# 544 tokens cut 256/288, with the high and low inputs of 256 tokens in one 512-column matmul

## Chip, cores and metric

One Trainium2 chip; the kernel runs on one of its cores. The metric is the device time of one execution in microseconds (us).

## What is computed

A trunk of two layers over 544 tokens (512 of a new stream, the prompt, and 32 of a running one, the sample), each of 1024 features, in float32:

```python
def layer(x, c, l, mixer):
    mods = (silu(c) @ ada_w[l] + ada_b[l]).reshape(c.shape[0], 9, D_MODEL)   # D_MODEL 1024
    h = modulated_pre(x, norm_pre[l, 0], mods, 0)          # rms_norm * (1 + scale) + shift
    x = gated_post(x, swiglu(h, w1, w3, w2), ...)          # D_FF 2816: (silu(h@w1) * (h@w3)) @ w2
    h = modulated_pre(x, norm_pre[l, 1], mods, 1)
    o, st = mixer(h, l)                                    # z = h @ w_in; latent attention | retention; @ w_out
    x = gated_post(x, o, norm_post[l, 1], mods, 1, 1.0)
    h = modulated_pre(x, norm_pre[l, 2], mods, 2)
    x = gated_post(x, swiglu(h, ...), ...)                 # a second FFN
```

## The kernel before

Activations lie feature-major: 128 features on the partitions, 8 tiles of them, 544 tokens along a row. A projection is made one output tile of 128 features at a time. To keep float32 precision with TensorE's faster float32r type, each operand is split into a high part (rounded to float32r) and a low part (the rest), and each product is three matmuls: high weights by high input, high weights by low input, low weights by high input. No matmul writes more than one PSUM bank of 512 float32, so the 544 tokens are cut in two halves of 272 (`HT`), which lie in two neighbouring banks. `tile3` does one step of 128 input features: six matmuls, `w_hi` by `hi` and `lo` for either half, then `w_lo` by `hi` for either half. In the up projection of the FFN and the mixer's input projection the second half has 276 columns (`HB`): the last four hold the adaLN shift of prompt and sample, so that the product with the shift comes out as a bias beside the tokens, to be added after the scaling with 1/rms (`rinv`).

The stages of a layer: FFN (44 up tiles in 22 features with two tiles each, w1 and w3; then 8 down tiles of 22 steps), mixer (21 input tiles z0 to z20, query projections, retention and attention, 8 output tiles), and a second FFN. Between stages lies a turn-over: the sum of squares of the output, its inverse root, the new x, the next h. The last output tile of a stage is made one token half after the other (`last_tile`), and the first two tiles of the next (`first_tiles`) start with the first half, so that the turn-over of one half lies beside the matmuls of the other. The halves are always the same 272 tokens.

Each engine has its own program, in an order written by hand, and they wait for each other on semaphores:

- SyncE's queue loads the weights of a tile into one of two slots of `raw`.
- ScalarE casts a slot to `w_hi` (L1176, L1183) when the tile before in that slot has been used, and GpSimd subtracts to get `w_lo` (`low`, L546). TensorE starts a tile when its `w_lo` is ready (`lo_done`) and says when it has used it (`w_used`).
- In the up projection, for each feature: when a tile is used, VectorE multiplies the 544 tokens out of PSUM by `rinv` (L1648, L1652) and copies the four bias columns (L1649, L1653). ScalarE takes the Silu of the first tile (L1300), VectorE makes the product (L1657), ScalarE casts it to `u_hi` (L1303), VectorE subtracts to get `u_lo` (L1662). The two features of a round have four banks each, so TensorE runs up to two tiles ahead.
- In the mixer's input projection, ScalarE's order for tile z is: cast of the high weights of tile z+2 (`high`), then `z_out` of tile z, which waits for VectorE's `z_scaled` of it (L1695, L1696). Between the `z_scaled` of z9 to z16 VectorE turns queries and keys by the rotary tables (L1726), in its order: four products, a `z_scaled`, eight sums, a `z_scaled`.
- The adaLN vectors of the next stages (L1561) are made on VectorE, most beside the down projection.
- The sums of squares are matmuls with a matrix or a column of ones (L679, L686). `apart_sb` of the change lies in `squares`, which holds partial sums of squares in the turn-overs.

Of the kernel before, what the change touches and what calls it, by code (L numbers as in the profile page):

```python
# [24 lines left out]
P = 128  # L25
# [4 lines left out]
HT = T // 2  # L30
TW = T + 4
HB = TW - HT
# [53 lines left out]

TOK_AT = [0, P, HT - P]
TOK = len(TOK_AT)
SUM_AT = HT + NS
# [24 lines left out]
def streaming_trunk(nc, a, o):  # L114
    ctx = ExitStack()
    with ctx:
# [24 lines left out]
        def signal(name, per_layer, before=0):  # L141
# [14 lines left out]
        rinv = sb("rinv", [P, T])  # L156
        squares = sb("squares", [P, T])
        ones = sb("ones", [P, P])
# [22 lines left out]
        tok_root = sb("tok_root", [P, 2 * TOK])  # L181
        tok_inv = sb("tok_inv", [P, 2 * TOK])
# [8 lines left out]
            [("h_hi", [P, KD, HP], F32R), ("h_lo", [P, KD, HP], F32R)],  # L191
# [6 lines left out]
            [("mla_hi", [P, 4, T], F32R), ("mla_lo", [P, 4, T], F32R),  # L198
             ("ret_hi", [P, 4, T], F32R), ("ret_lo", [P, 4, T], F32R)],
        ])  # L200
        sb("h_space", [P, size // 4])
        h_hi, h_lo, o_ffn, ada_w = hm["h_hi"], hm["h_lo"], hm["o_ffn"], hm["ada_w"]
        decay, mla_hi, mla_lo, ret_hi, ret_lo = hm["decay"], hm["mla_hi"], hm["mla_lo"], hm["ret_hi"], hm["ret_lo"]
# [3 lines left out]
            [("u_hi", [P, FT, T], F32R), ("u_lo", [P, FT, T], F32R)],  # L207
# [7 lines left out]
               [[("zq", [P, 2, T], F32), ("qn_hi", [P, 2, T], F32R), ("qn_lo", [P, 2, T], F32R)],  # L215
# [9 lines left out]
        u_hi, u_lo, kv, kpe, q_nope, q_pe = (um[n] for n in ("u_hi", "u_lo", "kv", "kpe", "q_nope", "q_pe"))  # L225
# [4 lines left out]
        qn_hi, qn_lo, state_p, k_tok = um["qn_hi"], um["qn_lo"], um["state_p"], hm["k_tok"]  # L230
# [13 lines left out]
        def pair(b):  # L244

            return ps[:, b:b + 2, 0:HT]

        def biases(b):

            return ps[:, b + 1, HT:HB]  # L250

        def halves(t):
            return t.rearrange("p (t n) -> p t n", t=2)

        def by_token(t):

            return ps[:, 5, SUM_AT + t * TOK:SUM_AT + (t + 1) * TOK]
# [29 lines left out]

        up_out = signal("up_out", 4 * FT, 4)
# [10 lines left out]

        z_mul = signal("z_mul", Z_C)  # L300
# [83 lines left out]
        def x_count(j, t, m):  # L384

            return 2 * KD * j + KD * t + m + 1

# [232 lines left out]
        def _(pe):  # L620
# [22 lines left out]
            def first_high(chunk):  # L643

                for t, w_t in enumerate((HT, HB)):
                    n = slice(t * HT, t * HT + w_t)
# [118 lines left out]
            def up(l, s):  # L765
# [3 lines left out]
                def feature(i, f, w):  # L769
                    pe.wait_ge(lo_done.sem, lo_done.at(l, base + i * 4 + 2 * f + w + 1))  # L770
                    for k in range(KD):
                        last = tile3(4 * f + 2 * w, w, k, h_hi[:, k, :], h_lo[:, k, :], k == 0, k == KD - 1, HB)
# [1296 lines left out]
```

## Time and profile before

| | us |
|---|---|
| median of 3 runs | 2362.61 (2362.09 to 2363.95) |
| span of the profiled execution, first to last instruction | 2360.0 |
| TensorE busy | 2304.0 (98%) |
| VectorE busy | 1220.4 (52%) |
| GpSimd busy | 880.6 (37%) |
| ScalarE busy | 821.1 (35%) |

The profile has no time of its own execution beside the span; the median of the runs is 2.6 us above it. Matmuls overlap in their records, so a busy TensorE is not one at its peak: what a matmul costs is the time from its start to the next one's. PE is TensorE's matmul, PEld its weight load, DVE VectorE, ACT ScalarE, POOL GpSimd; L546 is line 546 of the kernel. An engine's wait is the idle time in front of an instruction, with what ended it in brackets.

### The profile page before, as it was taken

The page shows a single profiled execution, that of the slowest core. Times are in us where ns is not written, and L with a number is a line of the kernel's source. Part 1 is how long each engine was busy: PE and PEld are TensorE (multiplying, and loading weights), DVE is VectorE, ACT ScalarE, POOL GpSimd, SP SyncE. Part 2 cuts the span into 40 slices and gives each one's busy share as a digit, 9 for nine tenths or more (in the row PEclk, how much of TensorE's full clock was granted, in tenths as well). Part 3 has the DMA queues.
Part 4 walks back from the last instruction along what each step waited for, and adds up shares of the span by engine and source line. Part 5 has one row for each costly group of instructions (what it writes and reads, how often), then busy time and mean ns, then how long its engine had stood idle before and what let it go on. Part 6 is the DMA issues. An engine that isn't in the chain of part 4 may idle for free.

```text
span 2360.0 us, 43873 instructions
## 1 busy us (share of the span) xinstructions
PE 2304.0 (98%) x17694; PEld 2184.5 (93%) x17694; DVE 1220.4 (52%) x2065; ACT 821.1 (35%) x1392; POOL 880.6 (37%) x382
## 2 busy tenths in 40 slices
PE   8999999999999999999999999999999999999998
PEld 7999999899558899999999999999984699999998
DVE  5333379877561533338153333996846624333502
ACT  4323332433454433332243333225343553332321
POOL 2344334343113344344434334443321143433352
PEclk7999999999999999999999999999999999999999
DMA  6222268322211122236312223882231022222422
GB/s 233 90 83 86 89 238 312 136 86 81 73 37 54 60 84 89 89 113 246 123 58 86 89 89 110 296 289 75 82 111 51 1 72 73 88 89 89 163 86 75
DMA packets 70948, 263.82 MB, mean 112 GB/s; under 512 B 8704, under 2 KB 10112, under 8 KB 70336
## 3 DMA queue, kind: packets, MB, share of 16 engines
q1 hardware_dynamic: 70848, 262.44, 33.1%
q8 instruction: 69, 1.13, 0.2%
q14 instruction: 31, 0.25, 0.0%
HBM read 258.96 MB, written 3.45 MB: 111 GB/s over the span
## 4 chain that ended last, share of the span: by engine, by line
PE 75%; issue 10%; DVE 5%; POOL 4%; ACT 3%; DMA 1%; SPq 1%; POOLq 0%; DVEq 0%; ACTq 0%
PE ps L673 21%; PE ps L669 20%; PE ps L670 20%; POOL w_lo L546 4%; DVE wide_v L1561 2%; PE ps L679 1%; PE ps L745 1%; PE ps L1090 1%; PE ps L832 1%; PE ps L834 1%; PE ps L833 1%; PE ps L975 1%; DMA x<-in_x 1%; PE ps L1113 1%; PE ps L1057 1%
## 5 line engine op out<-in xcount | busy, mean ns | idle before, releaser
L546 POOL TENSOR_TENSOR w_lo<-raw,w_hi 128x1024 fp32r<-128x1024 f32 (+1 forms) x304 | 785.9, 2585 | 1296.2 <-ACT w_hi L1183 947.4
L669 PE MATMUL ps<-h_hi,w_hi 128*128 128x272 f32 x3296 | 886.8, 289 | 3.7 <-POOL w_lo L546 3.7
L670 PE MATMUL ps<-h_lo,w_hi 128*128 128x272 f32 x3296 | 889.4, 287 | 0.0
L673 PE MATMUL ps<-h_hi,w_lo 128*128 128x272 f32 x3296 | 685.7, 289 | 0.0
L669 PEld LDWEIGHTS ps<-h_hi,w_hi 128*128 128x128 f32 x3296 | 619.1, 188 | 5.2 <-POOL w_lo L546 5.0
L670 PEld LDWEIGHTS ps<-h_lo,w_hi 128*128 128x128 f32 x3296 | 620.9, 188 | 0.2
L1183 ACT CAST w_hi<-raw 128x1024 fp32r<-128x1024 f32 (+1 forms) x236 | 269.3, 1141 | 830.6 <-PE ps L673 809.0
L673 PEld LDWEIGHTS ps<-h_hi,w_lo 128*128 128x128 f32 x3296 | 519.2, 188 | 0.0
L669 PE MATMUL ps<-u_hi,w_hi 128*128 128x272 f32 x1232 | 332.7, 288 | 1.0 <-POOL w_lo L546 1.0
L670 PE MATMUL ps<-u_lo,w_hi 128*128 128x272 f32 x1232 | 332.4, 289 | 0.0
L1561 DVE CUSTOM_DVE_ANT_0 wide_v<-ada_w,ps,ada_b 128x1024 bf16<-128x1024 f32 x256 | 309.0, 1285 | 22.7 <-DMA ada_w<-in_ada 18.2
L1652 DVE TENSOR_TENSOR wide_v<-ps,rinv 128x544 f32<-128x544 f32 x88 | 63.8, 725 | 437.3 <-PE ps L673 437.3
L673 PE MATMUL ps<-u_hi,w_lo 128*128 128x272 f32 x1232 | 255.2, 288 | 0.0
L1657 DVE SCALAR_TENSOR_TENSOR wide_v<-wide_v,wide_s 128x512 f32<-128x512 f32 (+1 forms) x176 | 193.7, 1139 | 105.2 <-ACT wide_s L1300 105.2
L669 PEld LDWEIGHTS ps<-u_hi,w_hi 128*128 128x128 f32 x1232 | 231.7, 188 | 1.9 <-POOL w_lo L546 1.9
L670 PEld LDWEIGHTS ps<-u_lo,w_hi 128*128 128x128 f32 x1232 | 232.1, 188 | 0.0
L673 PEld LDWEIGHTS ps<-u_hi,w_lo 128*128 128x128 f32 x1232 | 192.8, 188 | 0.0
L1303 ACT CAST u_hi<-wide_v 128x544 f32 (+1 forms) x88 | 57.1, 649 | 213.6 <-DVE wide_v L1657 213.6
L1587 DVE RECIPROCAL tok_inv<-tok_root 128x3 f32<-128x3 f32 x12 | 2.1, 176 | 247.4 <-ACT tok_root L1191 247.4
L1176 ACT CAST w_hi<-raw 128x1024 fp32r<-128x1024 f32 x68 | 71.2, 1047 | 125.5 <-PE ps L673 82.5
L1662 DVE TENSOR_TENSOR u_lo<-wide_v,u_hi 128x544 f32 x88 | 63.8, 726 | 80.1 <-ACT u_hi L1303 80.1
L1300 ACT ACTIVATE wide_s<-wide_s 128x512 f32<-128x512 f32 (+1 forms) x176 | 82.2, 514 | 4.6 <-DVE wide_s L1649 4.6
(284 smaller groups left out, 2642.3 us busy)
## 6 DMA issues: line engine op xcount, KB each, us to landing
raw<-in_w_up SPq DMA_DIRECT2D x176, 512.0 KB, 3.5
ada_w<-in_ada SPq DMA_DIRECT2D x128, 512.0 KB, 5.2
raw<-in_w_dn SPq DMA_DIRECT2D x64, 704.0 KB, 4.8
raw<-in_w_mix SPq DMA_DIRECT2D x64, 512.0 KB, 3.6
ada_first<-in_ada SPq DMA_DIRECT2D x10, 512.0 KB, 7.8
decay<-in_decay SPq DMA_DIRECT2D x2, 2048.0 KB, 8.7
ada_first<-in_ada_first SPq DMA_DIRECT2D x6, 512.0 KB, 11.4
x<-in_x SPq DMA_DIRECT2D x4, 544.0 KB, 17.2
```

The lines of the kernel that those rows point to most:

```text
L546: pool.tensor_tensor(w_lo[:, slot, 0:width], raw[:, slot, 0:width], w_hi[:, slot, 0:width].bitcast(F32), ALU.subtract).then_inc(lo_done.se ...
L669: pe.matmul(ps[:, bank + t, 0:width[t]], wh, hi[:, n], start=start, stop=False)
L670: pe.matmul(ps[:, bank + t, 0:width[t]], wh, lo[:, n], start=False, stop=False)
L673: last = pe.matmul(ps[:, bank + t, 0:width[t]], wl, hi[:, n], start=False, stop=stop)
L1176: nc.scalar.copy(w_hi[:, slot, 0:width], raw[:, slot, 0:width]).then_inc(hi_done.sem, 1)
L1183: nc.scalar.copy(w_hi[:, k, 0:width], raw[:, k, 0:width]).then_inc(hi_done.sem, 1)
L1300: nc.scalar.activation(wide_s[:, f, at], wide_s[:, f, at], ACT.Silu, bias=wide_s[:, f, T + 2 * v:T + 2 * v + 1]).then_inc(up_silu.sem, 1)
L1303: nc.scalar.copy(u_hi[:, bass.ds(i * 2 + f, 1), :].rearrange("p a n -> p (a n)"), tmp_v[:, f, :]).then_inc(up_hi.sem, 1)
L1561: v_.tensor_tensor_reduce(junk[v], ada_w[:, t, :], c_psum(v), 1.0, ada_b[:, b0 + t:b0 + t + 1], ALU.mult, ALU.add, mods[:, v, n0 + t:n0 + ...
L1652: v_.tensor_tensor(halves(tmp_v[:, f, :]), pair(4 * f + 2), halves(rinv[:, :]), ALU.mult)
L1657: v_.scalar_tensor_tensor(out=wide_v[:, f, at], in0=wide_v[:, f, at], scalar=wide_v[:, f, T + 2 * v:T + 2 * v + 1], in1=wide_s[:, f, at], ...
L1662: v_.tensor_tensor(u_lo[:, at, :].rearrange("p a n -> p (a n)"), tmp_v[:, f, :], u_hi[:, at, :].rearrange("p a n -> p (a n)").bitcast(F32) ...
```

## The change

The tokens are cut into 256 and 288 (`TA`, `TB`) everywhere. The two parts lie next to each other across a bank border: 256 in the upper half of bank b, 288 (or 292 with the four bias columns) from the start of bank b+1, so that all 544 or 548 columns are one contiguous stretch (`tokens`).

The high and low inputs are put into one tensor each (`h_both`, `u_both`, `qn_both`, `mla_both`, `ret_both`). In the up projection and in the mixer's input projection, after the first two tiles of a stage, a step is `tile3_apart`: one matmul of 512 columns multiplies the high weights with the high inputs of the 256 tokens, written to the lower half of bank b, and with their low inputs, written to the upper half; one of 256 columns adds the low weights by the high inputs to the lower half; then three of 292 columns for the other tokens. That is five matmuls for six. The lower half is added later: ScalarE copies it to `apart_sb` (after its cast of the next high weights), VectorE adds the copy to the upper half in PSUM (`add_apart`), waits for that, and multiplies all 548 columns at once by `rinv`, whose last four columns are ones; the copy of the bias columns goes away.

In the down, output and query projections a step stays six matmuls, three of 256 and three of 288, in the order of parts (`half3`). The first two tiles of a stage write their `w_lo` and high products of the 256 tokens to the lower half, and the low input's products to the upper half. The evacuations of the down and output tiles by ScalarE become one of 512 and one of 32 tokens, for three.

```diff
-HT = T // 2
+TA = 256
+TB = T - TA
-TOK_AT = [0, P, HT - P]
+TOK_AT = ((0, P), (0, P, TB - P))
...
+        rinv = sb("rinv", [P, TW])
+        apart_sb = squares[:, 0:2 * TA].rearrange("p (v n) -> p v n", v=2)
...
+        def part(b, t, more=0):
+            return ps[:, b + 1, 0:TB + more] if t else ps[:, b, 512 - TA:512]
+        def tokens(b, width=T):
+            return ps[:, b:b + 2, :].rearrange("p b n -> p (b n)")[:, 512 - TA:512 - TA + width]
+        def apart(b):
+            return ps[:, b, 0:TA]
...
-            def tile3(bank, slot, kk, hi, lo, start, stop, second=HT):
-                for t in range(2):
-                    n = slice(t * HT, t * HT + width[t])
-                    pe.matmul(ps[:, bank + t, 0:width[t]], wh, hi[:, n], start=start, stop=False)
-                    pe.matmul(ps[:, bank + t, 0:width[t]], wh, lo[:, n], start=False, stop=False)
-                for t in range(2):
-                    n = slice(t * HT, t * HT + width[t])
-                    last = pe.matmul(ps[:, bank + t, 0:width[t]], wl, hi[:, n], start=False, stop=stop)
+            def half3(bank, t, wh, wl, both, start, stop, more=0):
+                out, n = part(bank, t, more), slice(OFF[t], OFF[t] + WID[t] + (more if t else 0))
+                pe.matmul(out, wh, both[:, 0, n], start=start, stop=False)
+                pe.matmul(out, wh, both[:, 1, n], start=False, stop=False)
+                return pe.matmul(out, wl, both[:, 0, n], start=False, stop=stop)
+            def tile3_apart(bank, slot, kk, both, start, stop):
+                pe.matmul(ps[:, bank, :].rearrange("p (v n) -> p v n", v=2), wh, both[:, :, 0:TA], start=start, stop=False)
+                pe.matmul(apart(bank), wl, both[:, 0, 0:TA], start=False, stop=stop)
+                return half3(bank, 1, wh, wl, both, start, stop, 4)
...
@@ ScalarE, up projection @@
-                    for k in range(2) if ahead else ():
-                        high_at(l, base, i * 2 + f + 1, k, last_width if f else KD * P)
+                    for k in range(2):
+                        if ahead:
+                            high_at(l, base, i * 2 + f + 1, k, last_width if f else KD * P)
+                        else:
+                            used(l, base + k)
+                        nc.scalar.copy(apart_sb[:, k, :], apart(4 * f + 2 * k)).then_inc(up_apart.sem, 1)
@@ ScalarE, mixer @@
                 def z_out(z, buf, dst, func=ACT.Identity):
+                    used(l, MIX_C0 + z)
+                    nc.scalar.copy(apart_sb[:, buf, :], apart(z_bank(z))).then_inc(z_apart.sem, 1)
                     act.wait_ge(z_mul.sem, z_mul.at(l, z + 1))
@@ VectorE @@
+            def add_apart(b, slot, added, l, count):
+                v_.tensor_tensor(part(b, 0), part(b, 0), apart_sb[:, slot, :], ALU.add).then_inc(added.sem, 1)
+                dve.wait_ge(added.sem, added.at(l, count))
...
-                        dve.wait_ge(w_used.sem, w_used.at(l, FFN_C[s] + i * 4 + 2 * f + 1))
-                        v_.tensor_tensor(halves(tmp_s[:, f, :]), pair(4 * f), halves(rinv[:, :]), ALU.mult)
-                        v_.tensor_copy(wide_s[:, f, T:TW], biases(4 * f)).then_inc(up_out.sem, 1)
+                        dve.wait_ge(up_apart.sem, up_apart.at(l, 2 * n + 1))
+                        add_apart(4 * f, 0, up_added, l, 2 * n + 1)
+                        v_.tensor_tensor(wide_s[:, f, :], tokens(4 * f, TW), rinv[:, :], ALU.mult).then_inc(up_out.sem, 1)
```

## Rows read from the trace of the kernel before

**Rows 1.** The page, part 1: busy us (share of the span) and instructions.
```profile
PE 2304.0 (98%) x17694; PEld 2184.5 (93%) x17694; DVE 1220.4 (52%) x2065; ACT 821.1 (35%) x1392; POOL 880.6 (37%) x382
```

**Rows 2.** The page, part 4: shares of the chain that ended last.
```profile
PE ps L673 21%; PE ps L669 20%; PE ps L670 20%; POOL w_lo L546 4%; DVE wide_v L1561 2%; PE ps L679 1%; PE ps L745 1%; PE ps L1090 1%; PE ps L832 1%; PE ps L834 1%; PE ps L833 1%; PE ps L975 1%; DMA x<-in_x 1%; PE ps L1113 1%; PE ps L1057 1%
```

**Rows 3.** Windows: us; busy (count) PE, PEld, DVE, ACT, POOL; PEclk; DMA share, GB/s.
```profile
240.36:255.46 15.10, 15.10 (x122) 15.10 (x121) 6.64 (x10) 4.24 (x6) 5.50 (x3) 1.00 0.32 85
379.91:394.97 15.06, 15.06 (x122) 15.06 (x121) 15.06 (x25) 2.94 (x3) 6.26 (x4) 1.00 0.89 324
521.30:575.00 53.70, 52.50 (x415) 52.07 (x414) 52.09 (x62) 16.98 (x26) 20.52 (x8) 1.00 0.27 81
```

**Rows 4.** Waits of PE: total us, times, longest us.
```profile
PE ps L735 <- ACT h_hi L1201: 10.0, 15, 1.4
...
PE ps L669 <- POOL w_lo L546: 4.8, 8, 1.2
...
PE ps L832 <- POOL w_lo L546: 2.4, 4, 0.6
```

**Rows 5.** PE's timeline (start us, us) at two waits in the mixer.
```profile
565.04 0.39 PE L669 MATMUL ps<-h_hi,w_hi 128*128 128x272 f32 x1 [1.20 <-POOL w_lo L546]
...
578.15 0.39 PE L669 MATMUL ps<-h_hi,w_hi 128*128 128x272 f32 x1 [0.72 <-POOL w_lo L546]
```

**Rows 6.** Groups by line and form: count, busy us, mean ns, idle before.
```profile
L669 PE MATMUL ps<-h_hi,w_hi 128*128 128x276 f32 x1648 | 477.7, 290 | 0.0
...
L1657 DVE SCALAR_TENSOR_TENSOR wide_v<-wide_v,wide_s 128x512 f32<-128x512 f32 x88 | 179.4, 2038 | 105.2 <-ACT wide_s L1300 105.2
...
L1603 DVE TENSOR_TENSOR ps<-o_ffn,ps 128x272 f32<-128x272 f32 x64 | 28.2, 441 | 10.0 <-PE ps L711 10.0
...
L1330 ACT ACTIVATE o_ffn<-ps,mul_post 128x272 f32<-128x272 f32 x28 | 13.5, 483 | 37.0 <-DVE mul_post L1575 37.0
L1649 DVE COPY wide_s<-ps 128x4 f32<-128x4 f32 x88 | 13.4, 152 | 0.0
```

**Rows 7.** PE's timeline: float32 matmuls of 512 columns, and of one.
```profile
604.68 3.60 PE L920 MATMUL ps<-kv,k_tok 128*128 128x512 f32 x8
608.12 1.88 PE L930 MATMUL ps<-w_ukv,kv 128*128 128x512 f32 x4
...
775.40 0.81 PE L686 MATMUL ps<-ones,wide_s 128*128 128x1 f32 x6
776.07 0.37 PE L728 MATMUL ps<-h_hi,w_hi 128*128 128x272 f32 x1
```

**Rows 8.** Timeline of an up tile's evacuation.
```profile
201.30 1.05 ACT L1183 CAST w_hi<-raw 128x1024 fp32r<-128x1024 f32 x1 [4.91 <-PE ps L673]
...
202.43 2.39 POOL L546 TENSOR_TENSOR w_lo<-raw,w_hi 128x1024 fp32r<-128x1024 f32 x1 [3.56 <-ACT w_hi L1183]
...
203.31 2.22 DVE L1657 SCALAR_TENSOR_TENSOR wide_v<-wide_v,wide_s 128x512 f32<-128x512 f32 x2 [1.22 <-ACT wide_s L1300]
...
205.65 0.65 ACT L1303 CAST u_hi<-wide_v 128x544 f32 x1 [2.46 <-DVE wide_v L1657]
...
207.42 1.06 ACT L1183 CAST w_hi<-raw 128x1024 fp32r<-128x1024 f32 x1 [1.12 <-PE ps L673]
```

**Rows 9.** Timelines of DVE and POOL in the mixer's input projection.
```profile
521.34 0.72 DVE L1695 TENSOR_TENSOR z_tmp<-ps,rinv 128x544 f32<-128x544 f32 x1 [0.50 <-PE ps L673]
...
522.78 2.80 DVE L1726 TENSOR_TENSOR ret_q<-wide_v 32x544 f32<-32x544 f32 x1
...
535.51 0.72 DVE L1695 TENSOR_TENSOR z_tmp<-ps,rinv 128x544 f32<-128x544 f32 x1
...
572.93 0.72 DVE L1695 TENSOR_TENSOR z_tmp<-ps,rinv 128x544 f32<-128x544 f32 x1
...
522.47 2.54 POOL L546 TENSOR_TENSOR w_lo<-raw,w_hi 128x1024 fp32r<-128x1024 f32 x1 [3.47 <-ACT w_hi L1176]
...
535.05 2.82 POOL L546 TENSOR_TENSOR w_lo<-raw,w_hi 128x1024 fp32r<-128x1024 f32 x1 [4.16 <-ACT w_hi L1176]
```

More of the change, by code:

```diff
@@ L643, in first_high @@
             def first_high(chunk):
-                for t, w_t in enumerate((HT, HB)):
-                    n = slice(t * HT, t * HT + w_t)
+                for t in range(2):
+                    n = slice(TA, TW) if t else slice(0, TA)
                     if t:
@@ L656, in first_high @@
                                 pe.wait_ge(lo_done.sem, lo_done.at(0, chunk + w + 1))
[L657 removed]
+                            pe.matmul((part(2 * w, 1, 4) if t else apart(2 * w)), w_hi[:, w, k * P:(k + 1) * P], h_hi[:, k, n],
                                       start=k == 0, stop=False)
[L659 removed]
+                            pe.matmul((part(2 * w, 1, 4) if t else apart(2 * w)), w_lo[:, w, k * P:(k + 1) * P], h_hi[:, k, n],
@@ L664, in tile3 @@
+            def tile3(bank, slot, kk, both, start, stop):
                 wh = w_hi[:, slot, kk * P:(kk + 1) * P]
                 wl = w_lo[:, slot, kk * P:(kk + 1) * P]
-                width = (HT, second)
-                for t in range(2):
-                    n = slice(t * HT, t * HT + width[t])
-                    pe.matmul(ps[:, bank + t, 0:width[t]], wh, hi[:, n], start=start, stop=False)
-                    pe.matmul(ps[:, bank + t, 0:width[t]], wh, lo[:, n], start=False, stop=False)
@@ L676, in add_squares @@
             def add_squares(src, bank, start, stop, mat):
                 for t in range(2):
-                    last = pe.matmul(ps[:, bank + t, 0:HT], mat[:, :], src[:, t * HT:(t + 1) * HT],
-                                     start=start, stop=stop)
+                    last = pe.matmul(part(bank, t), mat[:, :], src[:, OFF[t]:OFF[t] + WID[t]], start=start, stop=stop)
                 return last
             def token_sums(src, t, start, stop):
-                for b, at in enumerate(TOK_AT):
-                    last = pe.matmul(by_token(t)[:, b:b + 1], src[:, t * HT + at:t * HT + at + P], ones[:, 0:1],
+                for b, at in enumerate(TOK_AT[t]):
+                    last = pe.matmul(by_token(t)[:, b:b + 1], src[:, OFF[t] + at:OFF[t] + at + P], ones[:, 0:1],
@@ L742, in first_tiles @@
                             pe.wait_ge(h_ready.sem, h_ready.at(l, ready_count(l, j, k)))
-                        for t, w_t in enumerate((HT, HB)):
-                            n = slice(t * HT, t * HT + w_t)
-                            last = pe.matmul(ps[:, 2 * w + t, 0:w_t], w_hi[:, w, k * P:(k + 1) * P], h_lo[:, k, n],
+                        for t in range(2):
+                            n = slice(TA, TW) if t else slice(0, TA)
+                            last = pe.matmul(part(2 * w, t, 4), w_hi[:, w, k * P:(k + 1) * P], h_lo[:, k, n],
                                              start=False, stop=k == KD - 1)
@@ L771, in feature @@
                     for k in range(KD):
-                        last = tile3(4 * f + 2 * w, w, k, h_hi[:, k, :], h_lo[:, k, :], k == 0, k == KD - 1, HB)
+                        last = tile3_apart(4 * f + 2 * w, w, k, h_both[:, :, k, :], k == 0, k == KD - 1)
                     last.then_inc(w_used.sem, 1)
@@ L860, in z_tile @@
                     for k in range(KD):
-                        last = tile3(bank, slot, k, h_hi[:, k, :], h_lo[:, k, :], k == 0, k == KD - 1, HB)
+                        last = tile3_apart(bank, slot, k, h_both[:, :, k, :], k == 0, k == KD - 1)
                     last.then_inc(w_used.sem, 1)
```

157 lines of the change are left out of this document (78 added, 79 removed).

## Prediction

> **What bounds the kernel now.** The page's busy table is read first [rows 1]: TensorE is busy 98% of the span, VectorE 52%, ScalarE 35%, GpSimd 37%. The chain that ended last agrees [rows 2]: the three matmul lines of `tile3` (L669, L670, L673) hold 61% of the span. A busy PE only says that matmuls follow each other, so the next question is what one costs, and that is read from start to start, not from the duration of one, which overlaps its neighbours. In the up projection 20 steps of the inner loop (a step is one call of `tile3`: six matmuls, three of 272 columns and three of 276) take from 240.36 to 255.46 us (the 122 counted are 120 and one cut at either end), so a step takes 755 ns, 125.8 a matmul; in the down projection, six of 272, 20 steps take 15.06 us, 753 ns, 125.5 a matmul [rows 3]. The clock is fully granted there (1.00, the 2.4 GHz level), and 1632 columns at 2.4 GHz are 680 ns: about 12 ns a matmul are spent beside its columns. The change can win only out of those 12 ns, since it streams the same columns: 512+256+3x292 = 1644 a step, as now.
>
> Second, where TensorE waits. The largest sum, 10.0 us, is in the turn-overs, on ScalarE, and 4.8 us are for the low weights of GpSimd [rows 4]. Of these the ones in the mixer's input projection matter here. Between 521.3 and 575 us VectorE is busy 52.1 of 53.7 us [rows 3]; it is the bound of that stretch, through ScalarE's order: `z_out` waits for VectorE's `z_scaled`, and the cast of the high weights of a later tile stands behind it, then GpSimd's low half, then the matmul. The end of it is seen at 565.04 and 578.15, where PE comes out of waits of 1.20 and 0.72 us [rows 5].
>
> **The change part by part.** (1) One matmul fewer per step, in all `tile3_apart` steps: by the count of a 276-column group [rows 6] 1648, of which 42 tiles x 8 x 4 = 1344 are in the up projections and 19 x 8 x 2 = 304 in the mixer. What the new widths cost is not in this trace and is bounded. A slope first: 12 more columns a step cost 2 ns, 0.17 ns a column; the clock alone would ask 0.42. I take the middle, 0.29: 292 columns 131.0 ns, 256 columns 120.6, 288 columns 130. For 512 columns two kinds of rows bound it. By kind, the same type with 12 ns beside the columns: 213.3+12 = 225.5. By length, eight float32 matmuls of 512 columns take 3.44 us, 430 ns each, which reads as two passes of 213.3 ns and 3 ns more [rows 7]: 216.5. I take 222, nearer to the row of the same type. A step is then 222+120.6+3x131.0 = 736 ns, 19 less than 755. The bounds: with a flat 12 ns for every matmul the step saves 11.5; with 216.5 and the slope of 0.17 (256 at 122.8, 292 at 128.9) it saves 29. In the up projections: 1344 x 19.4 = -26.1 us (-15.5 to -39).
>
> The Trainium skill, "TensorE: Matmul & The Clock Gate", section "Wait — 56ns, not 53.3ns?", says that a stream of warm matmuls costs its columns at 2.4 GHz and about 2.5 ns each. By it a step would take 700 ns, where the trace has 755, and a matmul fewer would save 1344 x 2.5 = 3.4 us. It fits the long float32 rows and not the rows of this type, so the sum goes by the rows.
>
> (2) 256/288 without the merge: down, output and query projections keep six matmuls a step, by the same slope from 125.5, 3x120.9+3x130.1 = 753, as now: nothing. The bounds are 0 (any straight line) and, if 256 columns take as long as 272, the fourth case below.
>
> (3) ScalarE gains 218 copies of 128x256 out of PSUM, about 0.45 us each (272 columns: 0.48 [rows 6]), 98 us on an engine at 35%. VectorE gains 218 adds of 0.43 us (a multiply of 272 columns out of SBUF and PSUM into PSUM, L1603, takes 0.44 [rows 6]) with a wait of about 0.1 on its own result, and loses as many copies of 0.15 (L1649): +0.36 us each, 78 us. In the up projections both are hidden. Tile ends at 201.2 us: ScalarE casts high weights 201.30 to 202.35, then the new copy to 202.8, VectorE's add and multiply to 204.1, where the multiply now ends at 202.0 (0.72 after the tile). But the product L1657 that follows takes 2.22 us now, lying beside GpSimd's w_lo (202.43 to 204.82) [rows 8]; VectorE's operations without PSUM are held while GpSimd runs. The new add and multiply read PSUM and fall into just that hold, so the product ends near 205.6 as it does now, and the cast of u_hi (205.65) and the next cast of high weights (207.42) stay. The cover: w_lo is ready at 204.8 for a tile that starts at 207.3, 2.4 us spare; a cost appears only when this is gone. Nothing, then.
>
> (4) The mixer's input projection. Here VectorE has no slack. From z9 (521.34) to z16 (572.93) eight tiles add 8 x 0.36 = 2.9 us, and z9 itself starts 1.6 us later behind cast and copy on ScalarE. Part is swallowed again: the rope product at 522.78 takes 2.80 us beside GpSimd's 522.47 to 525.0, while the multiply out of PSUM at 535.51 takes its 0.72 beside GpSimd's 535.05 to 537.87 [rows 9]. So z16 comes between 1.4 and 4.5 us later, counted from the end of tile 9; I take 2.4. PE's waits grow by this and by its own saving in those tiles, which is worth nothing. A layer: the seven tiles z2 to z8 save 7x8x0.0194 = 1.1, z19 and z20 0.3, the delay costs 2.4: +1.0, twice +2.0 us (0 to +6).
>
> (5) The turn-overs. VectorE updates x by two operations of 272 columns a tile (L1603 and L1605). With 288 in the second half each is about 16 ns longer (1 ns a column, from 0.72 us for 544 and 0.44 for 272 [rows 6, 9]): 2x8x16 ns = 0.27 us, in six turn-overs 1.6 us; the shorter first half lies ahead of a wait and gives nothing back. The last output tile waits for its second chunk's low weights in each FFN [rows 4]; behind that wait come 33 matmuls of 256 and 66 of 288: +0.15 us, four times 0.6. In the first FFN of a layer VectorE's adaLN products start after the last up tile's evacuation, which I put up to 0.3 us later, and the first sums of the last output tile wait for them: 0.25 a layer, 0.5. Together +2.7.
>
> **The sum.** -26.1+0+2.0+2.7 = -21.4 us. The profiled span is 2360.0 us and the median of the runs 2362.6; the 2.6 us around the span don't change, so the forecast is 2341 us.
>
> **The rivals.** *A flat cost per matmul*: every matmul carries 12 ns, the long one too. -15.5+2.5+2.7 = -10: 2352 us. For it: it is the plain reading of 755 and 753. Against: the slope of 0.17.
>
> *The load sets the pace*: each matmul has its own weight load, and 12 ns are what the load overhangs. Then the 512-column matmul hides it altogether and the slope stays 0.17: -39+1+2.7 = -35: 2327 us. For it: the slope, and the 3 ns of the long float32 rows [rows 7]. Against: with one column, where only the load is left, a matmul takes (776.07-775.40)/6 = 0.11 us, 112 ns [rows 7], so the load alone is not 125.
>
> *Time goes by the column*: the data type streams at 0.46 ns a column, and a matmul fewer gives only the 3 ns of [rows 7]. -3.4 to -4, mixer +4.5, turn-overs +2.7: +3, 2366 us, no change that can be told. Against: 12 columns should cost 5.5 ns and cost 2. The 2.5 ns of the Trainium skill's page would come out here too.
>
> *A floor under 272 columns* (the other side): 256 columns still take 125.5 ns, and wider ones pay the clock's 0.42. Then a merged step is 225.5+125.5+3x133 = 750, saving 5 ns, 6.7 us, and every step of the other projections is 3x125.5+3x132.2 = 773, 20 ns more, 864 steps (616 down, by the code, like the 112 output, 32 query and 104 of last tiles), +17.3 us. With mixer and turn-overs +7: +18, 2380 us. It decides from where the short matmul saves under 1 ns of the 6.7 that it should. Against: the one-column rows, 112 ns.
>
> **How the numbers follow.** A difference under about 0.2% (4.7 us) can't be told from none here. Chances: my forecast and what lies around it (2335 to 2347) 0.34; flat cost 0.22; load sets the pace 0.16; by the column 0.18; floor 0.10. The first three are faster by over 0.2%: 0.72. The column case falls mostly within it: 0.17 same; the floor and the rest of the column case 0.11 slower. The range leaves out the floor and the lower half of the load case: 2329 to 2367 us. The likeliest case alone: 2335 to 2347.
>
> **What the changed profile would show.** Step to step in the up projection about 736 ns, with starts 222 ns apart after the 512-column matmul, 121 after the 256, 131 after the 292; 753 in the down projection. The product L1657 well under its 2.04 us of now [rows 6]. No wait of PE for w_lo in the up projections. In the mixer waits on w_lo of 2 us and more where 1.20 and 0.72 stand now. Wrong would make it: a step near 750 (the short matmul or the column), waits of PE inside the up projections (part 3 has gone over its 2.4 us), or a mixer that grows by more than 6 us a layer.

## The result and the profile after

The changed kernel takes 2367.5 us (median of 20 runs; the kernel before, run beside it, 2363.8). The ratio is 1.0017, 95% interval 1.0010 to 1.0023. Run again later as an experiment of its own it came to 1.0028 (1.0017 to 1.0040). So it is 0.2 to 0.3% slower: no gain, and a loss so small that it is just told from no change. One of the 20 runs took 4445.7 us and does not enter the ratio. The forecast was 2341.

The page of the changed kernel, part 1, answers to [rows 1]:

```profile
PE 2300.9 (97%) x16016; PEld 2103.2 (89%) x16016; DVE 1231.0 (52%) x2066; ACT 872.6 (37%) x1568; POOL 881.2 (37%) x382
```

TensorE has 1678 matmul records fewer (1648 merged, 30 of sums and transposes at the turn-overs; a float32 matmul such as a sum leaves two records) and is busy almost as long as before. The matmuls are gone, and hardly any time came back. The windows below (us; busy and count of PE, PEld, DVE, ACT, POOL; clock; DMA) answer to [rows 3]; the first holds 20 steps of the up projection, the second 20 of the down projection, the third the end of the mixer's input projection, the last a stretch after a wait in it:

```profile
240.44:255.54 15.10, 15.10 (x102) 14.18 (x101) 6.71 (x10) 4.77 (x8) 5.51 (x3) 1.00 0.28 84
379.39:394.39 15.00, 15.00 (x122) 15.00 (x121) 14.78 (x25) 2.67 (x3) 6.44 (x3) 1.00 0.90 308
521.30:580.00 58.70, 55.90 (x368) 52.05 (x367) 53.98 (x64) 19.84 (x35) 21.74 (x9) 1.00 0.27 81
478.00:482.00 4.00, 4.00 (x19) 3.71 (x18) 1.16 (x2) 2.43 (x5) 2.38 (x1) 0.57 0.00 0
```

Twenty up steps of 5 matmuls take 15.10 us, 755.0 ns each: exactly the 755 of before with 6. Where the time is within a step is seen in PE's timeline (start, us):

```profile
240.44 0.39 PE L695 MATMUL ps<-h_both,w_hi 128*128 128x512 f32 x1
240.68 0.28 PE L696 MATMUL ps<-h_both,w_lo 128*128 128x256 f32 x1
240.79 0.29 PE L680 MATMUL ps<-h_both,w_hi 128*128 128x292 f32 x1
240.93 0.30 PE L681 MATMUL ps<-h_both,w_hi 128*128 128x292 f32 x1
241.06 0.30 PE L682 MATMUL ps<-h_both,w_lo 128*128 128x292 f32 x1
241.20 0.40 PE L695 MATMUL ps<-h_both,w_hi 128*128 128x512 f32 x1
```

The starts follow each other by 0.24, 0.11, 0.14, 0.13 and 0.14 us; the medians over all steps are 234, 117, 134, 137 and 135 ns, so 0.457 to 0.469 ns a column for every width. The forecast had 222, 121 and 131.

TensorE's waits (total us, times, longest), which answer to [rows 4]:

```profile
PE ps L758 <- ACT h_both L1218: 11.2, 18, 1.4
PE ps L695 <- POOL w_lo L561: 7.9, 6, 1.5
...
PE ps L680 <- POOL w_lo L561: 4.3, 8, 0.9
...
PE ps L695 <- DVE z_tmp L1724: 3.6, 2, 1.8
```

L695, the 512-column matmul, waits for low weights only in the mixer, three times a layer (the up projections have no such wait); the wait for z_tmp is new. Both are seen in the timeline of layer 0:

```profile
476.69 0.50 PE L695 MATMUL ps<-h_both,w_hi 128*128 128x512 f32 x1 [1.83 <-DVE z_tmp L1724]
...
554.96 0.50 PE L695 MATMUL ps<-h_both,w_hi 128*128 128x512 f32 x1 [1.25 <-POOL w_lo L561]
...
568.85 0.51 PE L695 MATMUL ps<-h_both,w_hi 128*128 128x512 f32 x1 [1.55 <-POOL w_lo L561]
...
582.35 0.50 PE L695 MATMUL ps<-h_both,w_hi 128*128 128x512 f32 x1 [1.14 <-POOL w_lo L561]
```

A stage, counted from its first matmul to the first of the next, changed like this (us, from the traces of both kernels; in brackets the second trace of the changed kernel):

| stage | before | after |
|---|---|---|
| mixer's input projection, layers 0 and 1 | 144.6, 144.2 | 149.9, 149.9 (149.7, 148.9) |
| up projections with the turn-over ahead (2nd to 4th) | 279.1, 277.4, 279.4 | 279.9, 278.2, 279.9 (279.7, 278.1, 279.4) |
| down projections (four) | 135.9, 135.9, 135.9, 138.3 | 134.8, 134.8, 136.0, 137.2 (135.2, 134.8, 134.8, 137.2) |
| output projections | 52.6, 52.6 | 51.8, 51.8 (52.0, 52.0) |

The mixer loses 11 us in the first trace, the up stages 2.2; down and output projections give 4.8 back. What lies between input and output projection, attention above all, took 1.8 us more in this one trace; with the same code a layer of it is 131.4 to 133.3 us long in the traces of the kernels here. Spans: 2360.0 before, 2370.5 and 2367.4 after: more than the medians' difference of 3.7 and 6.6 us, so the sums of stages say where the loss lies and the medians how large it is.

### The profile page after: what moved, and what is told of

Its sections match the earlier page's. It is cut to its first block, busy times and chain, and to the rows that moved or that the text cites. A ratio compares the mean times of both kernels' runs of the same rounds, so it can differ in the third digit from the quotient of the medians.

```text
span 2370.5 us, 40717 instructions
## 1 busy us (share of the span) xinstructions
PE 2300.9 (97%) x16016; PEld 2103.2 (89%) x16016; DVE 1231.0 (52%) x2066; ACT 872.6 (37%) x1568; POOL 881.2 (37%) x382
## 4 chain that ended last, share of the span: by engine, by line
PE 71%; issue 13%; DVE 6%; POOL 5%; ACT 3%; DMA 1%; SPq 1%; POOLq 0%; DVEq 0%; ACTq 0%
PE ps L695 14%; PE ps L682 13%; PE ps L680 13%; PE ps L681 13%; PE ps L696 7%; POOL w_lo L561 4%; DVE wide_v L1588 2%; PE ps L702 1%; PE ps L768 1%; PE ps L1108 1%; DVE ps L1629 1%; PE ps L993 1%; DMA x<-in_x 1%; PE ps L1075 1%; PE ps L1006 1%
## 5 line engine op out<-in xcount | busy, mean ns | idle before, releaser
L695 PE MATMUL ps<-h_both,w_hi 128*128 128x512 f32 x1648 | 654.9, 397 | 11.5 <-POOL w_lo L561 7.9
L681 PE MATMUL ps<-h_both,w_hi 128*128 128x292 f32 x1648 | 491.3, 298 | 0.0
L682 PE MATMUL ps<-h_both,w_lo 128*128 128x292 f32 x1648 | 490.5, 298 | 0.0
L680 PE MATMUL ps<-h_both,w_hi 128*128 128x292 f32 x1648 | 488.9, 297 | 0.0
L696 PE MATMUL ps<-h_both,w_lo 128*128 128x256 f32 x1648 | 460.1, 279 | 0.0
L680 PE MATMUL ps<-u_both,w_hi 128*128 128x256 f32 (+1 forms) x1408 | 404.9, 288 | 4.3 <-POOL w_lo L561 4.3
L681 PE MATMUL ps<-u_both,w_hi 128*128 128x256 f32 (+1 forms) x1408 | 406.2, 288 | 0.0
L682 PE MATMUL ps<-u_both,w_lo 128*128 128x256 f32 (+1 forms) x1408 | 405.5, 288 | 0.0
L680 PEld LDWEIGHTS ps<-h_both,w_hi 128*128 128x128 f32 x1648 | 309.5, 188 | 75.9
L695 PEld LDWEIGHTS ps<-h_both,w_hi 128*128 128x128 f32 x1648 | 310.1, 188 | 13.7 <-POOL w_lo L561 9.3
L696 PEld LDWEIGHTS ps<-h_both,w_lo 128*128 128x128 f32 x1648 | 310.9, 189 | 0.2
L682 PEld LDWEIGHTS ps<-h_both,w_lo 128*128 128x128 f32 x1648 | 310.8, 189 | 0.0
L681 PEld LDWEIGHTS ps<-h_both,w_hi 128*128 128x128 f32 x1648 | 310.1, 188 | 0.0
L680 PEld LDWEIGHTS ps<-u_both,w_hi 128*128 128x128 f32 x1408 | 264.8, 188 | 6.1 <-POOL w_lo L561 6.1
L682 PEld LDWEIGHTS ps<-u_both,w_lo 128*128 128x128 f32 x1408 | 264.9, 188 | 0.0
L681 PEld LDWEIGHTS ps<-u_both,w_hi 128*128 128x128 f32 x1408 | 264.8, 188 | 0.0
```

The lines of the kernel that those rows point to most:

```text
L680: pe.matmul(out, wh, both[:, 0, n], start=start, stop=False)
L681: pe.matmul(out, wh, both[:, 1, n], start=False, stop=False)
L682: return pe.matmul(out, wl, both[:, 0, n], start=False, stop=stop)
L695: pe.matmul(ps[:, bank, :].rearrange("p (v n) -> p v n", v=2), wh, both[:, :, 0:TA], start=start, stop=False)
L696: pe.matmul(apart(bank), wl, both[:, 0, 0:TA], start=False, stop=stop)
```

## The experiments

The first questions were whether the long matmul is worth anything, and what of the loss is the mixer's. Edits are against the changed kernel unless another is named; every step length below is the median over stretches of 20 steps without a wait, at a granted clock of 1.00.

**Two matmuls for the long one.**

```
-  pe.matmul(ps[:, bank, :].rearrange("p (v n) -> p v n", v=2), wh, both[:, :, 0:TA], ...)
+  pe.matmul(apart(bank), wh, both[:, 0, 0:TA], ...)
+  pe.matmul(part(bank, 0), wh, both[:, 1, 0:TA], ...)
```

> The changed kernel with its 512-column matmul cut into two of 256 (high inputs to the lower half of the bank, low inputs to the upper), six matmuls a step again, all else as changed. Theory A, time goes by the column (256 columns 117 ns, 512 columns 234 in the changed trace): a step stays at 756 to 758 ns and the ratio to the kernel before at 1.0017, within 0.0015. Theory B, a flat 12 ns a matmul is there and the 512-column matmul is slow for another reason (its two-part operand, or a whole bank written): a step is 234-2x119 = 4 ns shorter or up to 12 ns longer, and in the second case the ratio goes to 1.010.

Measured: 2367.3 us, ratio 1.0024 (1.0014 to 1.0033), as the changed kernel. The step is 755.0 ns with six matmuls as with five. A matmul fewer gives nothing in these steps, not even 3 ns.

**The merge undone in the mixer alone.** There `tile3` with 256/292 columns, no copy and no add.

```
-  last = tile3_apart(bank, slot, k, h_both[:, :, k, :], k == 0, k == KD - 1)
+  last = tile3(bank, slot, k, h_both[:, :, k, :], k == 0, k == KD - 1, 4)
-  nc.scalar.copy(apart_sb[:, buf, :], apart(z_bank(z))).then_inc(z_apart.sem, 1)
-  add_apart(bank, z % 2, z_added, l, z + 1)
```

> The changed kernel with the merge undone in the mixer's input projection only: six matmuls a step (256/292) into their places, no copy on ScalarE, no add on VectorE; the up projections stay merged. Theory A, the whole loss is the mixer's chain (input projection 144.6 us before, 149.9 as changed): it falls to 143.5 to 144.8 us in either layer, and the ratio to the kernel before to 0.997 to 0.9985. Theory B, the loss is the uneven token halves (turn-overs) and the slower clock of wide matmuls: the mixer's input projection stays above 147 us and the ratio above 1.0005.

Measured: 2360.3 us, 0.9989 (0.9980 to 0.9999). The input projection is back at 144.2 and 144.3 us and the up projections stay as they were: the loss is the mixer's, some 7 us of it by the medians.

**Widths swept in the down projection.** A step has three matmuls of one width, 32 to 256, and then three of another, 304 to 512 (columns left out, or added from other tokens, so the products are others).

```
+  first = (256, 32, 64, 96, 128, 160, 192, 208, 224, 240, 256)[kk]
+  second = (512, 304, 320, 352, 384, 416, 448, 464, 480, 496, 512)[kk]
```

> The changed kernel with other widths in the down projection, where a step has three matmuls of one width and then three of another: 32 to 256 columns and 304 to 512. It leaves part of the down product's tokens out and adds columns that belong to other tokens, so only starts in the trace are read. Theory A (by the column): from about 256 up the start-to-start time is 0.457 to 0.463 ns a column, 512 at 234; below, a floor of 107 to 112 ns (the weight load). Theory B (a flat cost): a line of 0.417 ns a column plus 12, so 320 at 145.5 and 512 at 225. Theory C (a load that overhangs): flat at about 117 under 256, and 216 at 512 where the output is one stretch.

PE's timeline of this kernel, at 512 and at 32 columns:

```profile
319.64 0.40 PE L698 MATMUL ps<-u_both,w_hi 128*128 128x512 f32 x1
319.87 0.40 PE L699 MATMUL ps<-u_both,w_hi 128*128 128x512 f32 x1
320.11 0.39 PE L700 MATMUL ps<-u_both,w_lo 128*128 128x512 f32 x1
...
321.38 0.18 PE L698 MATMUL ps<-u_both,w_hi 128*128 128x32 f32 x1
321.41 0.26 PE L699 MATMUL ps<-u_both,w_hi 128*128 128x32 f32 x1
321.52 0.26 PE L700 MATMUL ps<-u_both,w_lo 128*128 128x32 f32 x1
```

The median from the second to the third matmul of a width: 110 to 112 ns from 32 to 224 columns, then 113.5 at 240, 117 at 256, 139 at 304, 163 at 352, 195 at 416, 210 at 464 and 232.5 at 512. (The first and second of a narrow group start closer together, 26 ns apart at 32 columns and 59 at 128, and those of the wide group behind it farther apart by as much, so that a whole step takes three times either median.) That is a floor, at the 112 ns that one column takes in [rows 7], and above it a line through the origin: 0.453 to 0.469 ns a column, 0.454 at 512. With 256 columns and more nothing is left that a longer matmul could save. The duration that the row gives (0.40 at 512) is not this time: it overlaps its neighbours.

**Types.** In the same place the operands are also read as float32 (the same bits), or replaced by bf16 constants (so the products are others).

```
+  kind = "rbbbrrrfffr"[kk]          # r float32r, b bf16, f float32
+  if kind == "f":
+      wh, wl, hi, lo = (t.bitcast(F32) for t in (wh, wl, hi, lo))
```

> The changed kernel with other data types in steps of the down projection: bf16 (weights and inputs a constant tile), float32r and float32 (the same bits), each at 128, 192, 256, 292, 384 and 512 columns; the down product is not the reference's. Theory A, the extra tenth belongs to float32r: float32r 0.457 ns a column (512 at 234), bf16 0.417 ns a column plus 2.5 (512 at 216), float32 two passes at 0.417 (512 at 430). Theory B, it belongs to accumulating into PSUM or to three matmuls into one place: bf16 and float32r alike at 0.457, float32 at 0.457 a pass (512 at 468).

Rows of the timeline: bf16 with 512 columns, float32r with 512, float32 with 292 (float32r is shown as f32 too; float32 is known by the x2, since each of its matmuls leaves two records):

```profile
313.04 0.38 PE L713 MATMUL ps<-ones 128*128 128x512 bf16 x1
313.25 0.38 PE L714 MATMUL ps<-ones 128*128 128x512 bf16 x1
313.47 0.38 PE L715 MATMUL ps<-ones 128*128 128x512 bf16 x1
...
315.64 0.40 PE L713 MATMUL ps<-u_both,w_hi 128*128 128x512 f32 x1
315.87 0.40 PE L714 MATMUL ps<-u_both,w_hi 128*128 128x512 f32 x1
316.11 0.39 PE L715 MATMUL ps<-u_both,w_lo 128*128 128x512 f32 x1
...
317.00 0.66 PE L713 MATMUL ps<-u_both,w_hi 128*128 128x292 f32 x2
317.50 0.66 PE L714 MATMUL ps<-u_both,w_hi 128*128 128x292 f32 x2
317.99 0.66 PE L715 MATMUL ps<-u_both,w_lo 128*128 128x292 f32 x2
```

Medians: bf16 56 ns at 128 columns, 82 at 192, 109 at 256, 126 at 292, 216 at 512: the columns at 2.4 GHz and 2 to 4 ns. Float32, from record to record: 246 at 292 and 429 at 512, twice the bf16 times to within 6 ns, and with two records the matmul takes 0.49 us at 292, as the starts 317.00, 317.50 and 317.99 show: four times bf16. Float32r: 120 at 256 and 235 at 512. The tenth above the clock's 0.417 ns a column belongs to float32r and grows with the columns; it does not come from adding up in PSUM, which all three do, nor from reading these tensors, which the float32 matmuls read too. (The bf16 matmuls read a small constant tile of ones.) The Trainium skill's "TensorE: Matmul & The Clock Gate", section "Wait — 56ns, not 53.3ns?", says columns and about 2.5 ns a matmul: the bf16 rows agree with it (56 and 216 ns), the float32r rows do not (235).

**No merge anywhere**, tokens 256/288: the changed kernel's layout of banks, `tile3` for every projection, no copies and no adds.

> The changed kernel with the merge undone everywhere: three pairs of matmuls of 256 and 288 (292) columns in every projection, and none of ScalarE's copies and VectorE's adds; what is left of the change is the split of the tokens. Theory A (the merge gives nothing, its copies and adds are hidden in the up projections): the stages of the up projections stay within 1 us of those of the changed kernel (278.3 to 279.9 us), the mixer's input projection is 144.2 to 144.6 us as without the merge there, and the time is 0.998 to 1.000 of the kernel before. Theory B (the copies and adds still cost the up projections something, by ScalarE's and VectorE's queues at the turn-overs): each up stage gives 1 us or more back and the time is 0.996 to 0.998.

Measured: 2359.2 us, 0.9986 (0.9977 to 0.9995); input projections 144.0 and 144.8, up stages 279.2, 278.4 and 279.1. It agrees with A: 176 copies and adds in the up projections cost next to nothing (2360.3 with them; the three up stages are 1.4 and 0.5 us longer in all in the two traces of the changed kernel). Of the kernels that leave nothing out this is the fastest.

**The same with 272/272.** `TA = 272`, three token sums in each half.

> The kernel without the merge, its tokens split 272/272 again in the new layout of the banks (the two halves lie side by side over two banks), with three sums by token in each half. Theory A (time goes by the column, so the split is worth nothing where only matmuls run, and the shorter down and output stages come from one single-column sum and one transpose fewer for the first half): up stages within 0.3 us of the kernel with 256/288, down stages back from 134.8 to 135.8 us and output stages from 51.8 to 52.6, mixer's input projection 144.2 to 144.6, the time 0.999 to 1.001 of the kernel before. Theory B (256 columns beside 288 are themselves cheaper than twice 272): up stages 1 us or more longer than with 256/288 as well, the time 0.5 per thousand or more above it beyond the down stages' part.

Measured: 2366.7 us, 1.0019 (1.0010 to 1.0028). Down stages 135.5 to 135.6 and output stages 52.5, as A said; but the up stages are 280.5, 278.5 and 280.5, and the total above A's. B's sign is right: in this order and this layout 256/292 is cheaper than 272/276. The window says by how much (this kernel, then the one with 256/288, 20 up steps each):

```profile
240.81:255.98 15.17, 15.17 (x123) 15.17 (x121) 6.51 (x8) 4.23 (x6) 5.47 (x3) 1.00 0.26 87
```

```profile
240.98:256.08 15.10, 15.10 (x123) 15.10 (x122) 6.38 (x9) 4.71 (x7) 4.81 (x2) 1.00 0.28 102
```

758.3 against 755.0 ns. The kernel before, with the same 272/276, has 755.0; but it issues both low-weight matmuls last, where the change groups all three of a half. Hence the next two.

**The new order in the kernel before** (edit against that kernel):

```
     for t in range(2):
         pe.matmul(ps[:, bank + t, 0:width[t]], wh, hi[:, n], ...)
         pe.matmul(ps[:, bank + t, 0:width[t]], wh, lo[:, n], ...)
-    for t in range(2):
         last = pe.matmul(ps[:, bank + t, 0:width[t]], wl, hi[:, n], ...)
```

> The kernel before with one edit, the order of the six matmuls of a step: high, low and low-weight matmul of the first half, then the three of the second half, where before has the two low-weight matmuls last. The kernel with 272/272 in the new layout takes 758.3 ns a step in the up projections, the kernel before 755.0. Theory A (the order makes the 3.3 ns: the same output is then written three times in a row): 758 ns a step, 1344 steps are 4.4 us, the time 1.0015 to 1.002 of the kernel before. Theory B (the place of the first half in its bank, columns 240 to 511, or the joined buffer makes it): 755 ns, the time 0.9995 to 1.0005.

Measured: 2366.6 us, 1.0017 (1.0008 to 1.0026). The time is A's, the reason only in part: the up step is 755.9 (+0.9), the down step 756.6 (+3.3).

**The old order in the kernel without a merge**, 256/288:

> The kernel with 256/288 and without the merge, with the order of before in each step (both low-weight matmuls last). Theory A (the order costs 3.3 ns a step whatever the widths): 752 ns a step in the up projections, 1344 x 3.3 = 4.4 us less there and 1 to 3 us in the down and output projections, the time 2352 to 2355 us, 0.996 to 0.9975 of the kernel before, which would be the fastest here. Theory B (the widths 256 and 288/292 gain the 3.3 ns over 272 and 272/276 by themselves, the order does nothing): 755 ns, the time as without the edit, 0.9986.

Measured: 2367.2 us, 1.0016 (1.0007 to 1.0025): neither. The up step grows to 760.0, the down step from 750.0 to 753.3. What order, widths and layout do together:

| ns a step | up and mixer | down |
|---|---|---|
| 272/272, low weights last (before) | 755.0 | 753.3 |
| 272/272, by halves, in before | 755.9 | 756.6 |
| 272/272, by halves, new layout | 758.3 | 751.6 |
| 256/288, low weights last | 760.0 | 753.3 |
| 256/288, by halves | 755.0 | 750.0 |
| 256/288, by halves, merged (after) | 755.0 | 750.0 |

Each length held in all stages of a trace, but for the kernels with 256/288 by halves: there a whole down or output stage may stand at 753.3 or an up stage at 756.6. In the two traces of the changed kernel it was the third down stage in one, the first down stage and both output stages in the other. So the same 1644 columns take 755 to 760 ns a step, and the same 1632 columns 750 to 757, by the pattern of widths, order and place in the banks and sometimes by the execution. No straight line in the columns gives that, and I have no mechanism for it.

**The mixer: both early copies first.** ScalarE's copy of z1 goes ahead of z0's output and its square.

```
+  z_copy(0)
+  z_copy(1)
   def z_out(z, buf, dst, func=ACT.Identity):
-      used(l, MIX_C0 + z)
-      nc.scalar.copy(apart_sb[:, buf, :], apart(z_bank(z))).then_inc(z_apart.sem, 1)
+      if z >= 2:
+          z_copy(z)
```

> The changed kernel with one edit in ScalarE's program of the mixer: the copy of the apart products of z1 is issued right behind that of z0, ahead of z0's output and the first square, where it stands behind both in the changed kernel. Theory A (that order makes TensorE's wait of 1.83 us before z3): this wait falls under 0.5 us, the mixer's input projection from 149.9 to about 148 us, the time 3 to 4 us under the changed kernel's, 1.0000 to 1.0005 of the kernel before. Theory B (VectorE's chain alone sets both, the wait only moves): input projection 149.5 to 150, the time as of the changed kernel, 1.0017.

Measured: 2363.0 us, 1.0002 (0.9993 to 1.0010), 4.6 us below the changed kernel's median; input projection 146.1 and 146.8. The wait for z_tmp is gone. The chain that made it stands in the changed kernel's timeline of ScalarE, VectorE and TensorE:

```profile
473.52 0.72 ACT L1373 ACTIVATE zq<-z_tmp 128x512 f32<-128x512 f32 x1 [3.36 <-DVE z_tmp L1724]
...
474.15 0.30 ACT L1374 ACTIVATE zq<-z_tmp 128x32 f32<-128x32 f32 x1
...
474.49 0.66 ACT L1378 ACTIVATE wide_s<-zq 128x544 f32<-128x544 f32 x1
...
475.05 0.35 ACT L1371 COPY squares<-ps 128x256 f32<-128x256 f32 x1
475.44 0.43 DVE L1575 TENSOR_TENSOR ps<-ps,squares 128x256 f32<-128x256 f32 x1 [1.95 <-ACT squares L1371]
475.90 0.73 DVE L1724 TENSOR_TENSOR z_tmp<-ps,rinv 128x548 f32<-128x548 f32 x1
476.67 0.72 ACT L1373 ACTIVATE zq<-z_tmp 128x512 f32<-128x512 f32 x1 [1.26 <-DVE z_tmp L1724]
```

z1's copy starts 1.5 us after z_out(0) began, VectorE has waited 1.95 us for it, and the tile that takes z1's banks starts at 476.69 only, 1.83 us late. The edit brought back twice that in layer 0 (3.7 us; 3.1 in layer 1). The rest is the clock. Windows of 2 us behind the wait, in the changed kernel:

```profile
476.00:478.00 2.00, 1.31 (x8) 1.23 (x9) 0.63 (x1) 1.30 (x3) 0.00 (x0) 1.00 0.04 8
478.00:480.00 2.00, 2.00 (x10) 1.90 (x9) 0.44 (x2) 1.50 (x3) 0.70 (x1) 0.55 0.00 0
480.00:482.00 2.00, 2.00 (x10) 1.81 (x10) 0.72 (x1) 0.93 (x2) 1.69 (x1) 0.59 0.00 0
482.00:484.00 2.00, 2.00 (x15) 1.86 (x15) 0.00 (x0) 0.00 (x0) 0.00 (x0) 1.00 0.53 188
```

Soon after the pause the granted clock fell from its upper level to the lower one, 1.2 GHz, for most of 4 us: 2.00 x 0.45 + 2.00 x 0.41 = 1.7 us lost. In the second trace of the changed kernel layer 0 has the fall too (0.50 and 0.67), but layer 1 has the same wait and no fall:

```profile
1639.80 0.50 PE L695 MATMUL ps<-h_both,w_hi 128*128 128x512 f32 x1 [1.83 <-DVE z_tmp L1724]
```

```profile
1640.00:1642.00 2.00, 2.00 (x14) 1.86 (x14) 0.00 (x0) 1.97 (x4) 0.00 (x0) 1.00 0.00 0
1642.00:1644.00 2.00, 2.00 (x15) 1.86 (x14) 1.16 (x2) 0.74 (x3) 1.57 (x1) 1.00 0.00 0
```

The kernel with two 256-column matmuls has the wait of 1.8 us in both layers and a clock of 1.00 behind it. So of six such waits three were followed by the fall, both layers of the first trace among them. From the end of this wait to the end of the next one, for low weights, it was 78.3 us with the fall and 76.8 without, which prices the fall at 1.5 us. The z1 copy costs a layer 1.8 us without it and 3.3 to 3.5 with it.

**The mixer without VectorE's add** (the low inputs' products are left out of its first 256 tokens; copy and waits stay).

```
-  add_apart(bank, z % 2, z_added, l, z + 1)
```

> The changed kernel without VectorE's add in the mixer; ScalarE's copy and the waits for it stay. It leaves the products of the low inputs out of the first 256 tokens of the mixer's input projection. Theory A (the 0.43 us of each add stretches VectorE, which is the bound between z9 and z16): the mixer's input projection falls from 149.9 to 145 to 147.5 us, TensorE's waits for the low weights there fall from 1.25, 1.55 and 1.14 us to the 1.20 and 0.72 of before. Theory B (the delay is the way over ScalarE, where the copy stands behind other work and VectorE waits for it): input projection above 148.5 us. If A, the time is 0.998 to 1.0003 of the kernel before, if B 1.001 or more.

Measured: 2360.0 us, 0.9986 (0.9977 to 0.9995), input projection 145.4 and 145.9. That is A. The waits of TensorE from 444 us to the end of that stage:

```profile
PE ps L758 <- ACT h_both L1218: 2.3, 4, 1.4
PE ps L695 <- POOL w_lo L561: 2.1, 3, 1.1
PE ps L695 <- DVE z_tmp L1723: 0.9, 1, 0.9
```

The changed kernel has 3.9 for w_lo and 1.8 for z_tmp there. The add is 1.8 us of the first, and half of the second. That makes 2.7 of the 4.5 us that layer 0 gained; the other 1.8 is mainly the clock, which did not fall behind the shorter wait (1.00 in the windows from 476 to 484 us). So A's range was met with the help of something that A did not name.

**Both edits in the mixer.**

> The changed kernel with both edits in the mixer: the two copies ahead of z0's output, and no VectorE add; the products of the low inputs are left out of the first 256 tokens of the mixer's input projection. Theory A (copy order and add are the whole loss, and each hides behind the other in part, since one alone brought 149.9 to 146.1 and 145.4 us): input projection 144.0 to 144.6 us as without the merge. Theory B (the way over ScalarE's copy costs by itself): 145 us or more in both layers.

Measured: 2359.5 us, 0.9987 (0.9977 to 0.9996); input projection 144.9 and 144.8. Between A and B, nearer to A: the order of the copies and the add are nearly the whole loss. Against the kernel with the mixer unmerged (144.2 and 144.3) 0.7 and 0.5 us stay. Of this 0.2 is a longer wait for low weights (2.1 us a layer for 1.9); the rest is a wait for the low inputs in the turn-over (0.4 and 0.2 us), which the kernel with no merge anywhere has too in its second layer. So no more than 0.2 us a layer is shown to come from ScalarE's copies.

**The changed kernel again.**

> The changed kernel once more, unedited, for a second profile of it. Its first profile has a span 2.4 us above what the median of its runs leaves for it. If the input projection of the mixer is a fixed order of waits, it is 149.9 us again in both layers; if it varies from execution to execution it may be 148.5 as in the kernel with two matmuls of 256 columns.

Measured: 2368.8 us, ratio 1.0028 (1.0017 to 1.0040), input projection 149.7 and 148.9. The waits are fixed (1.83 to 1.86 us for z_tmp, 3.9 for low weights); the microsecond that varies is mainly the clock, which did not fall in layer 1.

## Why the prediction was wrong

**Part 1, the term that carried the forecast (-26.1 us), is 0.** The failed step is the first reading: "about 12 ns a matmul are spent beside its columns". 755 ns for 1632 or 1644 columns does not say whether the surplus over the clock belongs to the matmul or to the column. The slope that I took for the answer, 2 ns for 12 columns more, came from two different stages, the up and the down projection. The table of steps shows steps of the same number of columns differing by 5 to 7 ns, by order, widths and place, so that slope was no measurement of a column. The 512-column matmul was priced at 222 ns and takes 234. The price leaned on the float32 rows of [rows 7], and float32 runs at another rate than float32r. These rows were also misread: the x8 are the two records each of four matmuls, so that 430 ns is half a matmul (likewise the six records of one column are three matmuls). Even the upper bound, 225.5, was low. What the runs showed in its place: float32r costs 0.46 ns a column from 256 columns up and nothing for the matmul itself; the step is 755.0 ns with five matmuls and with six. The rival "time goes by the column" had this mechanism, at 0.46 ns. That its 2366 us is so near to 2367.5 is partly luck: it counts 3.4 to 4 us for fewer matmuls, where nothing came, and 4.5 us for the mixer, where 7 to 11 came, and leaves out what the next parts gain. Its one objection, "12 columns should cost 5.5 ns and cost 2", is the same false slope.

**Part 2 was put at nothing and is not quite nothing.** Down and output steps went from 753.3 to 750.0 in 8 of the 12 such stages of the changed kernel's two traces (query steps were not measured): -2.5 us if all 760 did, -1.9 and -1.5 as they stood. The bound "any straight line gives 0" did not hold, as the steps follow none. The new order of the six matmuls I had not seen as a change at all; by itself it costs (+4.5 us in the kernel before); with the new widths and layout it is the old order that costs (about +8 us).

**Part 3 was right.** The product that follows the new add and multiply now takes 1433 ns, where [rows 6] have 2038:

```profile
L1685 DVE SCALAR_TENSOR_TENSOR wide_v<-wide_v,wide_s 128x512 f32<-128x512 f32 x88 | 126.1, 1433 | 3.1
...
L1575 DVE TENSOR_TENSOR ps<-ps,squares 128x256 f32<-128x256 f32 x218 | 94.1, 432 | 601.8 <-ACT squares L1318 530.5 <-ACT squares L1371 69.8 <-DVE rinv L1666 1.0
...
L1318 ACT COPY squares<-ps 128x256 f32<-128x256 f32 x176 | 63.7, 364 | 0.0
L1371 ACT COPY squares<-ps 128x256 f32<-128x256 f32 x42 | 15.2, 361 | 0.0
```

In the tile that [rows 8] show, the cast of the high inputs starts at 205.75 where it stood at 205.65. The add is 0.43 as taken; the copy is 0.36, not 0.45. TensorE has no wait for low weights there, and the kernel with copies and adds in the up projections (0.9989 of before) is as fast as the one without (0.9986).

**Part 4 was right in its delay and missed a second wait.** The waits for w_lo grew from 1.9 to 3.9 us a layer; the forecast delay was 2.4. But +1.0 a layer became +5.3 and +5.7 in the first trace (+5.1 and +4.7 in the second). Of the difference, 1.1 + 0.3 is the saving that does not exist, and 1.8 is a wait at the other end of the stage: I followed VectorE from z9 on, where it is saturated, and did not ask what ScalarE's new copy of z1 stands behind, and who waits for the banks of z1. Another 1.5 to 1.7 is the clock after this wait, where it fell. "A mixer that grows by more than 6 us a layer" was the bound given; it came close to it.

**Part 5, +2.7, was never measured by itself, and a gain was overlooked.** Not counted were the sums and transposes by token: 256 tokens need two blocks of 128 where 272 needed three, which takes 30 records away, 3.4 us at 112 ns each ([rows 7]). The stages bear this out: a down stage that kept its 753.3 ns a step went from 135.9 to 135.2 us. The kernel without a merge is 3.6 us faster than before by the medians; its down and output steps, as they stood in its trace, give 1.5, and the records 3.4, which leaves 1.3 us for the longer second half. In that trace the up stages behind turn-overs are 0.8 us longer in all than before and the mixer's input projections as long as before. So the term is nearer to 1 us than to 2.7, within what medians and single traces can tell.

The sum by what was measured, from before to after: -3.6 for the kernel without a merge, 0 to 1 for the merge in the up projections, and the mixer's 7 to 11 make +3 to +8; the two comparisons gave +3.7 and +6.6.

What stays open: why six matmuls of the same columns take 5 to 7 ns more or less by order, widths and place, and what decides whether the lower clock follows the wait of 1.8 us (three times of six).

## What to carry to other kernels

Whether a matmul's surplus over the clock is paid for each instruction or for each column can't be read from one width; two widths from the same stage and the same type are needed, and a float32 row says nothing of float32r. Before merging matmuls, look whether they are longer than their load: above it there was nothing to merge away. When an evacuation gets a second engine, look at each place in that engine's queue at which the new instruction stands, not only at the stretch that is full, and at who reuses the bank.

## What the runs showed that was not expected

- Float32r took 0.453 to 0.469 ns a column from 256 columns up, 7 to 9% more than bf16 of the same width (117 for 109 ns at 256, 232.5 to 235 for 216 at 512). Weight load and matmul of float32r together never came under 110 to 112 ns, in repeated matmuls of one width; bf16 came to 56. A float32 matmul took 0.49 us at 292 columns, four times bf16 and 3.6 times float32r.
- A pause of 1.8 us was followed by the lower clock for most of 4 us in three of six cases, which nearly doubled its price.
- Order, widths and place of six matmuls with the same columns in all moved a step by 5 ns (1644 columns) and 7 ns (1632), and the same code took 750.0 or 753.3 ns in different stages of one execution.
